# Expert stage of a 32-expert layer: the down bias is summed once from the gate table, turned h goes ahead of the turned rows, and the next expert's bias is added between them

## The reference

```python
gates = jax.nn.softmax(top_vals, axis=-1)            # 4 of 32 per token
gu = xb @ w_gu[e] + b_gu[e]                          # 1024 -> 2048
gate = jnp.minimum(gu[:, :D_FF], SWIGLU_LIMIT)
up = jnp.clip(gu[:, D_FF:], -SWIGLU_LIMIT, SWIGLU_LIMIT)
h = (up + 1.0) * (gate * jax.nn.sigmoid(SWIGLU_ALPHA * gate))
y_row = h @ w_down[e] + b_down[e]                    # 1024 -> 1024
y = segment_sum(y_row * gate_of_row, token)
x = layernorm(DEEPNORM_ALPHA * x + y, ln2_g, ln2_b)
```

## Time and profile before

| | us |
|---|---|
| median of 3 runs (lowest, highest) | 1252.86 (1252.75, 1255.14) |
| the profiled execution, its own time | 1254.36 |
| its span in the profile | 1252.6 |
| mean granted clock of TensorE | 0.985 |

### The profile page before, as it was taken

How to read it: one execution, slowest core, us unless ns; L and a number is a source line. 1 busy time by engine, 2 the same in 40 slices (tenths; PEclk the granted TensorE clock), 3 DMA queues, 4 the chain that set the end, 5 groups by cost and what they waited for, 6 DMA issues and landing times.

```text
span 1252.6 us, 14341 instructions
## 1 busy us (share of the span) xinstructions
PE 1192.6 (95%) x5761; PEld 564.6 (45%) x5761; DVE 521.7 (42%) x988; ACT 252.9 (20%) x392; POOL 13.4 (1%) x16
## 2 busy tenths in 40 slices
PE   9999999998999999999999998999999999999992
PEld 8989999563333333333333332333333333333330
DVE  5887788563223322223333222322332222333326
ACT  4645646111111111111111111111111111111101
POOL 1000000000000000000000000000000000000003
PEclk9999999999999999999999999999999999999986
DMA  9756645856999999999999999999999999999951
GB/s 246 233 185 208 195 134 152 322 204 269 384 422 421 421 420 421 421 420 421 422 421 421 421 420 422 421 421 421 421 420 422 422 420 421 421 421 421 421 226 42
DMA packets 120186, 443.73 MB, mean 354 GB/s; under 512 B 10824, under 2 KB 68312, under 8 KB 70974
## 3 DMA queue, kind: packets, MB, share of 16 engines
q1 hardware_dynamic: 120030, 442.69, 88.9%
q10 hardware_dynamic: 96, 0.22, 0.0%
HBM read 441.34 MB, written 1.53 MB: 354 GB/s over the span
## 4 chain that ended last, share of the span: by engine, by line
PE 79%; DVE 11%; ACT 7%; issue 3%; DMA 1%; DVEq 0%; POOL 0%; ACTq 0%; POOLq 0%
PE PS L758 36%; PE PS L790 18%; PE PS L699 7%; PE PS L614 5%; PE PS L632 2%; PE PS L707 2%; PE PS L714 2%; DVE w_lo L827 2%; PE PS L752 2%; DVE tiles L865 2%; ACT mid L526 2%; ACT mid L530 2%; ACT mid L548 1%; PE PS L785 1%; DVE tiles L929 1%
## 5 line engine op out<-in xcount | busy, mean ns | idle before, releaser
L758 PE MATMUL PS<-ring,mid 128*64 128x512 f32 x2048 | 447.6, 595 | 0.0
L758 PEld LDWEIGHTS PS<-ring,mid 128*64 128x64 f32 x2048 | 144.4, 137 | 286.9 <-issue 286.9
L790 PE MATMUL PS<-ring,mid 128*64 128x512 f32 x1024 | 230.6, 603 | 0.0
L1121 DVE TENSOR_SCALAR PS<-PS 128x512 f32<-128x512 f32 x32 | 22.4, 699 | 384.5 <-PE PS L758 384.5
L614 PE MATMUL PS<-x_hi,w_hi 128*128 128x320 f32 x448 | 141.7, 316 | 3.8 <-DVE w_lo L827 3.8
L1108 DVE TENSOR_TENSOR ys<-PS,ys 64x512 fp32r<-64x512 f32 x64 | 44.1, 689 | 235.3 <-ACT ys L551 234.9
L614 PE MATMUL PS<-x_hi,w_lo 128*128 128x320 f32 x448 | 139.1, 310 | 0.0
L614 PE MATMUL PS<-x_lo,w_hi 128*128 128x320 f32 x448 | 139.0, 310 | 0.0
L790 PEld LDWEIGHTS PS<-ring,mid 128*64 128x64 f32 x1024 | 71.6, 139 | 139.3 <-issue 139.3
L865 DVE SCALAR_TENSOR_TENSOR x_tok<-PS,gate,x_tok 128x1024 f32<-128x1024 f32 (+1 forms) x96 | 122.9, 1281 | 27.4 <-PE PS L721 24.3
L543 ACT ACTIVATE mid<-PS 128x512 f32<-128x512 f32 x32 | 19.1, 597 | 454.6 <-DVE PS L1121 454.6
(11 more groups left out here) (195 smaller groups left out, 700.1 us busy)
## 6 DMA issues: line engine op xcount, KB each, us to landing
ring<-in_w_gu SPq DMA_DIRECT2D x256, 1024.0 KB, 20.9
ring<-in_w_down SPq DMA_DIRECT2D x128, 1024.0 KB, 20.9
raw<-in_w_in SPq DMA_DIRECT2D x56, 512.0 KB, 5.2
ring<-in_w_out SPq DMA_DIRECT2D x4, 1024.0 KB, 6.1
x_tok<-in_x_prompt SPq DMA_DIRECT2D x1, 1024.0 KB, 6.9
out<-x SPq DMA_DIRECT2D x2, 512.0 KB, 2.6
bias_raw<-in_b_gu SPq DMA_DIRECT2D x4, 128.0 KB, 3.2
ln_g<-in_ln_g SPq DMA_DIRECT2D x1, 512.0 KB, 4.1
```

Source lines behind the costliest of these rows:

```text
L758: last = mm(PS[64 * a:64 * a + 64, b, :], xgT[:, u % 4, u // 4, :], w[:, o:o + HALF], start=False, stop=(u == KC - 1))
L790: last = mm(PS[64 * a:64 * a + 64, XB, :], hT[:, 2 * (u % 2) + j, u // 2, :], w[:, j * D + a * HALF:j * D + (a + 1) * HALF], start=False, ...
```

## The change

- The matmul of down bias in each expert goes (L785), and the down product starts its sum with its own first matmul. For it, `gate4` (four copies of the gate table) is written by VectorE before the routing's list of extra blocks is formed, turned by TensorE (three transposes) and split in a high part `gT_hi` (ScalarE) and a low part `gT_lo` (VectorE). In expert 0, where there is nothing to combine, `gated_bias` multiplies it with b_down, four matmuls for each of the three tiles, and `begin` on VectorE writes ALPHA times x1 plus that product into `y_acc`.
- `turn_h` comes ahead of `turn_x`. `turn_x` now waits for ScalarE's copy of turned h, which goes to `th` itself.
- `add_bias` for the next expert stands between the two turns and not at the head of the expert, except for experts 0, 14 and 16 (`ALONE`).
- `keep_busy` before and after the first `turn_x` goes; the wait for posT moves into expert 0, behind its gate/up product; the register loads of TensorE, ScalarE and VectorE move behind expert 13.
- VectorE does three adds in every expert, expert 0 among them, so the counts of `c_done` and `c_taken` move by three.

```diff
             def one_expert(i, it):
 
                 s, n = i % 2, UNITS * i
+
+                def sum_up(t):
+
+                    if i == 0:
+                        gated_bias(t, CB[t])
+                    else:
+                        combine(t, 1 - s, CB[t])
+
                 pe.wait_ge(xgT_ok, 2 * it + rows_in(i))
-                sel = esel4[:, s].rearrange("p a r -> p (a r)")
-                for b in range(2):
-                    mm(PS[:, b, :], sel, bias4[:, b, :], start=True, stop=False)
+                if i in ALONE:
+                    add_bias(s)
...
-                if i > 0:
-                    if i > 1:
-                        pe.wait_ge(c_taken, 6 * it + 3 * (i - 1))
+                if i == 0:
+                    pe.wait_ge(gT_ok, 2)
+                else:
+                    pe.wait_ge(c_taken, 6 * it + 3 * i)
                     pe.wait_ge(ohT_ok, 2 * it + i)
-                    combine(2, 1 - s, CB[2])
+                sum_up(2)
                 pe.wait_ge(ohT_ok, 2 * it + (i + 1))
-                if i + 1 < NE:
-                    pe.wait_ge(xg_ok, 2 * it + (rows_in(i) + 1))
-                    turn_x(xg_sb, tx_done)
-                if i > 0:
-                    combine(1, 1 - s, CB[1])
-                if i + 1 < NE:
-                    pe.wait_ge(xgT_ok, 2 * it + (rows_in(i) + 1))
                 pe.wait_ge(h_ok, 2 * it + (i + 1))
                 turn_h(th, ht_done)
-                if i > 0:
-                    pe.wait_ge(c_taken, 6 * it + (3 * (i - 1) + 1))
-                    combine(0, 1 - s, CB[0])
+                sum_up(1)
+                if i + 1 < NE:
+                    if i + 1 not in ALONE:
+                        add_bias(1 - s)
+                    pe.wait_ge(xg_ok, 2 * it + (rows_in(i) + 1))
+                    pe.wait_ge(hT_ok, 2 * it + (i + 1))
+                    turn_x(xg_sb, tx_done)
+                pe.wait_ge(c_taken, 6 * it + (3 * i + 1))
+                sum_up(0)
                 pe.wait_ge(hT_ok, 2 * it + (i + 1))
-                mm(PS[:, XB, :], sel, bias4[:, 2, :], start=True, stop=False)
```

and the new product:

```diff
+            def gated_bias(t, bank):
+
+                t0, n = TILES[t]
+                for a in range(2):
+                    rows = slice(64 * a, 64 * a + 64)
+                    mm(PS[0:n, bank + a, :], gT_hi[rows, t0:t0 + n], bias4[rows, 2, :], start=True, stop=False)
+                    last = mm(PS[0:n, bank + a, :], gT_lo[rows, t0:t0 + n], bias4[rows, 2, :], start=False, stop=True)
+                last.then_inc(c_done, 1)
```

More of the change, by code:

```diff
@@ L27 @@
 LOOP = 14
+ALONE = (0, LOOP, LOOP + 2)
 AHEAD = 3
@@ L196, in hybrid_layer @@
         xg_sb, xgT_f = (mid[:, i * HALF:(i + 1) * HALF] for i in range(2))
-        th = mid[:, 4 * HALF:5 * HALF]
         ys = place("ys", [P, 2, HALF], MID + 8 * HALF, F32R)
@@ L203, in y_rows @@
             return ys[first:first + ROWS, a, :]
-        hT_f = xg_sb
+        th = mid[:, 4 * HALF:5 * HALF]
+        hT_f = th
+        gT_hi = place("gT_hi", [P, T], MID + 8 * HALF, F32R)
+        gT_lo = place("gT_lo", [P, T], MID + 8 * HALF + 4 * T, F32R)
+        gate4 = mid[:, 4 * HALF - 3 * P:4 * HALF].rearrange("p (t h e) -> p t h e", t=3, h=4)
         xgT = xgT_f.rearrange("p (j a r) -> p j a r", j=4, a=2)
@@ L255, in hybrid_layer @@
         pos_ok, pos_turned, posT_ok = sem("pos_ok"), sem("pos_turned"), sem("posT_ok")
+        g4_ok, gate_turned, gT_ok = sem("g4_ok"), sem("gate_turned"), sem("gT_ok")
         tab_ok, tab_done, items_ok = sem("tab_ok"), sem("tab_done"), sem("items_ok")
@@ L535, in _ @@
             act.activation(posT4[:, :], PS[:, 6, 0:T], ACT.Copy).then_inc(posT_ok, 1)
-            act.wait_ge(items_ok, 1)
-            n_loop = act.value_load(pairs[0:1, 0:1], min_val=1, max_val=1 + MAX_EXTRA // 2)
-            n_more = act.value_load(pairs[0:1, 1:2], min_val=0, max_val=MAX_EXTRA // 2)
+            act.wait_ge(gate_turned, 1)
+            act.activation(gT_hi[:, :], PS[:, 7, 0:T], ACT.Copy).then_inc(gT_ok, 1)
             def one_expert(i, it):
@@ L545, in one_expert @@
                     take_xg(2 * it + (rows_in(i) + 1))
-                    take_xgT(2 * it + (rows_in(i) + 1))
                 act.wait_ge(ht_done, 2 * it + (i + 1))
                 act.activation(hT_f, PS[:, TB, :], ACT.Copy, scale=0.5).then_inc(hT_ok, 1)
+                if i + 1 < NE:
+                    take_xgT(2 * it + (rows_in(i) + 1))
                 act.wait_ge(used, 2 * UNITS * it + UNITS * (i + 1))
@@ L554, in _ @@
                 one_expert(i, 0)
+            act.wait_ge(items_ok, 1)
+            n_loop = act.value_load(pairs[0:1, 0:1], min_val=1, max_val=1 + MAX_EXTRA // 2)
+            n_more = act.value_load(pairs[0:1, 1:2], min_val=0, max_val=MAX_EXTRA // 2)
             with act.Fori(0, n_loop) as it:
@@ L725, in _ @@
             gather(1)
+            pe.wait_ge(g4_ok, 1)
+            for t, (t0, n) in enumerate(TILES):
+                last = pe.transpose(PS[:, 7, t0:t0 + n], gate4[0:n, t], ident[0:n, 0:n])
+            last.then_inc(gate_turned, 1)
             pe.wait_ge(tab_ok, 1)
@@ L731, in _ @@
             last.then_inc(tab_done, 1)
-            keep_busy(2, 1)
             pe.wait_ge(xg_ok, 1)
             turn_x(xg_sb, tx_done)
-            keep_busy(2, 1)
             pe.wait_ge(pos_ok, 1)
@@ L744, in unit, with chosen, add_bias @@
                 return ring[:, n % SLOTS, :]
+            def chosen(par):
+                return esel4[:, par].rearrange("p a r -> p (a r)")
+            def add_bias(par):
+                for b in range(2):
+                    mm(PS[:, b, :], chosen(par), bias4[:, b, :], start=True, stop=False)
+            def gated_bias(t, bank):
[5 more added lines that the diff above has]
+                last.then_inc(c_done, 1)
             def one_expert(i, it):
                 s, n = i % 2, UNITS * i
+                def sum_up(t):
[3 more added lines that the diff above has]
+                        combine(t, 1 - s, CB[t])
                 pe.wait_ge(xgT_ok, 2 * it + rows_in(i))
-                sel = esel4[:, s].rearrange("p a r -> p (a r)")
-                for b in range(2):
-                    mm(PS[:, b, :], sel, bias4[:, b, :], start=True, stop=False)
+                if i in ALONE:
+                    add_bias(s)
                 for u in range(KC):
@@ L760, in one_expert @@
                     last.then_inc(used, 1)
-                mm(PS[:, TB, 0:T], sel, posT4[:, :], start=True, stop=True).then_inc(spread_done, 1)
+                if i == 0:
+                    pe.wait_ge(posT_ok, 1)
+                mm(PS[:, TB, 0:T], chosen(s), posT4[:, :], start=True, stop=True).then_inc(spread_done, 1)
                 if i > 0:
@@ L791, in one_expert @@
                                       w[:, j * D + a * HALF:j * D + (a + 1) * HALF],
-                                      start=False, stop=(u == 3 and j == 1))
+                                      start=(u == 0 and j == 0), stop=(u == 3 and j == 1))
                     last.then_inc(used, 1)
+            for i in range(LOOP):
+                one_expert(i, 0)
             pe.wait_ge(items_ok, 1)
@@ L797, in _ @@
             n_more = pe.value_load(pairs[0:1, 1:2], min_val=0, max_val=MAX_EXTRA // 2)
-            pe.wait_ge(posT_ok, 1)
-            for i in range(LOOP):
-                one_expert(i, 0)
             with pe.Fori(0, n_loop) as it:
@@ L811, in _ @@
             pe.wait_ge(ylo_ok, 2 * n_more + NE)
-            pe.wait_ge(c_taken, 6 * n_more + 3 * (NE - 1))
+            pe.wait_ge(c_taken, 6 * n_more + 3 * NE)
             for t, b in LAST_SUMS:
@@ L1059, in _ @@
             last.then_inc(pos_ok, 1)
+            dve.tensor_copy(gate4, gate[:, :, :].unsqueeze(2).to_broadcast([P, 3, 4, NE])).then_inc(g4_ok, 1)
             link(dve.tensor_scalar(ext, cnt, float(ROWS), None, ALU.is_gt))
@@ L1096, in part, with begin @@
                 return dve.value_load(items[0:1, 1, ds(i, 1)], min_val=0, max_val=NB)
[L1098 to L1102, removed]
+            def begin(t, count, bank):
+                n = TILES[t][1]
+                dve.wait_ge(c_done, count)
+                return stt(halves(y_acc[0:n, t, :]), halves(x1[0:n, t, :]), ALPHA, PS[0:n, bank:bank + 2, :],
+                           ALU.mult, ALU.add)
             def low_part(count):
@@ L1114, in one_expert @@
                 s = i % 2
-                if i > 0 and i != LOOP + 2:
+                if i == 0:
+                    dve.wait_ge(gT_ok, 1)
+                    dve.tensor_tensor(gT_lo[:, :], PS[:, 7, 0:T], gT_hi[:, :].bitcast(F32), ALU.subtract)\
+                       .then_inc(gT_ok, 1)
+                elif i != LOOP + 2:
                     low_part(2 * it + i)
@@ L1127, in one_expert @@
                 stt(th, up, 1.0, th, ALU.add, ALU.mult).then_inc(h_ok, 1)
-                if i > 0:
-                    for q, t in enumerate((2, 1, 0)):
-                        add(t, before, 6 * it + (3 * (i - 1) + q + 1), CB[t]).then_inc(c_taken, 1)
```

(13 more changed lines are left out.)

## The result

The changed kernel takes 1241.78 us in the median of four runs (1238.89 to 1242.78), the kernel before 1252.80 (1252.06 to 1255.14): 0.9905 of it by all its executions, interval 0.9883 to 0.9927. That is 11.0 us less by the medians and 11.9 by the ratio, where 17.4 were forecast. The median lies 0.3 us above the upper end of the forecast's range, 1241.5; 0.9905 of the 1252.86 that the forecast stood on is 1241.0, just inside it, and the interval runs from 1238.2 to 1243.7, across that end. The two profiled executions differ by more than the medians do: 1254.36 and 1241.01 us, spans 1252.6 and 1239.2, so 13.4 us.

A forecast was written before the change was run, and what follows sets the result against it. TensorE and the weight transfers both run at full load, TensorE living on a shrinking lead. Terms -14.4 - 0.8 - 1.6 - 0.6 = -17.4 us, from 1252.86 to 1235.5 us; range 1232.5 to 1241.5.

The forecast's parts named there:

- the lead, 14.4 us: At unit 379, last gate/up unit: TensorE's remaining lead over the weight transfers, read from bytes moved; pays out -14.4 us.
- the semaphore's release: At unit 379's landing: a small deduction that takes the lead from 14.6 to 14.4 us.
- The start, -0.8: Before the experts: the expert stage begins earlier despite gate4's extra copy; -0.8 us, bounds -1.3 and +0.5.
- The hole in expert 0, -1.6: Expert 0's transfer gap: gated_bias keeps TensorE busy, no clock fall, first down unit earlier; -1.6 us, bounds 0 and -2.7.
- The last expert, -0.6: Last expert, which has no gather: only the down bias matmul L785 goes; -0.6 us.
- The rule against it: Paced experts: by the Trainium skill's HAM oscillation rule, TensorE idling 0.78 us per gate unit would run them at a throttled clock.
- the second rival: Paced experts: the clock stays down, 52 us an expert; two whole experts give 1279 us; chance 3%.
- the first rival: After unit 379: its matmuls at half speed (+1.7) and all down matmuls at 1.2 GHz (+4.2), 1241.4 us; chance 12%.
- its signs: What would show it: last ring transfer near 1207.5, 421 GB/s, late experts 29.9 us, ring waits 30 to 45 us.

## Why the prediction was right and wrong

**Right: what bounds the kernel, and what stays of the gain.** That TensorE lives on a lead, that it would save 42 to 60 us and that only the lead would be paid out was the core of the forecast. TensorE's expert fell to 27.02 us (26.9 to 27.5 was said). Matmuls idle for the ring 30.7 us (30 to 45 was said), most late experts take 29.8 us (the transfers' 29.9 was said; two take 30.1 and 31.1), the rate stays 421, and with lighter transfers 46 us that were waits for weights come back as time saved. The lead is gone at expert 12, a little before the 14 to 20 that were said; the loop after expert 15, which the prediction left out, gives part of it back.

**Wrong in size: the lead, 14.4 us.** This is the step that failed. I took the landing of unit 379 from the bytes moved. What TensorE waits for is the last of its packets, on the slowest of the 16 DMA engines, and the mean of the engines is ahead of that one: in the kernel before the 16 landing marks of unit 379 come from 1190.8 to 1198.2, on average at 1195.0. A row of the kernel before that I didn't read had the answer: the times from issue to landing of the last two gate units, issued at 1168.2 and 1172.2.

```profile
DMA to landing us min/median/max: 26.0/26.7/27.5
```

The 27.5 belongs to the unit issued at 1168.2, the 26.0 to the last one. So unit 379 landed at 1198.2, and the lead was 1208.9 - 1198.2 = 10.7 us. Between the two executions unit 379's matmuls moved from 1208.9 to 1197.6, 11.2 us: the lead of 10.7 and 0.6 by which its landing came earlier (1197.6). The prediction's term is 3.7 us too large, and that is most of the 4.0 us that the forecast has too much on the spans (17.4 against 13.4). The 0.2 us it took off for the semaphore's release are 0.04 in the chain above (landed at 1197.59, used at 1197.63).

**The start, -0.8: not seen.** Its own piece is right in kind. From the product of the list of blocks to the first bias matmul 1.59 us pass (287.01 to 288.60), where 2.79 did:

```profile
286.44 0.57 PE PS L736 x3
287.01 0.23 PE PS L741 x4
...
287.95 0.60 ACT mid L535
...
288.60 0.73 PE PS L763 x2
```

But that product came 1.2 us later: 0.57 are the three new transposes, the rest lies before the change's first line. The prediction had the transposes on an idle TensorE; there is no such gap, since they follow the gather, which ends at 286.43, and the product follows them. Over the twelve profiled executions the first gate/up matmul comes anywhere between 287.8 and 294.8, and a run bound by the transfers carries each of these microseconds to its end. An effect of 0.8 can't be told in that; in the two executions that are compared here both begin the gate/up product at 289.3.

**The hole in expert 0, -1.6: -1.4 there, -0.6 at the end.** The stretches of the earlier trace rows, after:

```profile
305.00:310.00 5.00, 5.00 (x28) 2.48 (x26) 3.87 (x5) 1.62 (x3) 0.00 (x0) 1.00 1.01 426
310.00:315.00 5.00, 5.00 (x26) 1.73 (x26) 1.22 (x1) 0.17 (x1) 0.00 (x0) 1.00 0.95 364
315.00:320.00 5.00, 5.00 (x26) 1.63 (x24) 2.07 (x6) 1.18 (x2) 0.00 (x0) 1.00 1.00 341
```

TensorE is busy in the first, the clock doesn't fall in the second, and the loss is (57 + 80) x 5 = 0.69 MB or 1.6 us where it was 2.7. Unit 32 lands at 329.4, where it landed at 330.7: 1.4 us earlier. By unit 379 only 0.6 of that is left (1197.6 against 1198.2); where the rest went the traces don't say. All nine executions with gated_bias in expert 0 keep the clock there, and the three without it lose it.

**The last expert, -0.6: -0.5**, from unit 379's first matmul to the first down matmul. Not in the sum: the down stage 1.1 us shorter, since the clock fell for 3.4 us there and not for 6.8, and the tail 0.5 shorter, which I can't place. The first is luck: with three units in flight the kernel before had 3.4 us of fall there too. The sum as measured, on the spans: -10.7 (lead) - 0.6 (transfers) - 0.5 - 1.1 - 0.5 = -13.4. The 2.4 us between that and the medians' 11.0 is the scatter of single runs: this profiled run before stood 1.6 over its median, that of after 0.8 under.

**The rule against it.** TensorE did idle about 0.5 us before each paced unit, and over 100 us of paced experts the page of stretches says:

```profile
1100.00:1200.00 100.00, 92.14 (x412) 30.78 (x410) 26.50 (x39) 10.71 (x18) 0.00 (x0) 1.00 1.01 421
```

The granted clock is 1.00, so the second rival did not come true. The Trainium skill's warning on HAM oscillation (TensorE: Matmul & The Clock Gate) is of tiles of matmuls that are shorter than the wait between them. The prediction held the matmuls (1.71 us) against the whole transfer (2.49 us) and not against the wait. The wait is 0.5 us and so shorter than the matmuls: the paced experts don't meet the page's condition, and no run here tests its rule. The clock does fall, from 736.6 to 746.9, at the loop after expert 15, where TensorE has idled for 2.9 us before it.

The range, by the medians, missed by 0.3 us. Its upper end, 1241.5, was the price of the first rival, the clock down at the end. That the measured 1241.8 comes so near it is luck: unit 379's matmuls ran at a granted clock of 1.00 (1.94 us with their modelled ends) and the down stage took 8.3 us, not 13.7. The lead, on which most of the sum stood, was given no bounds of its own. And the prediction put the last ring unit at 1205.3 in its sum and near 1207.5 among its signs; it landed at 1207.5, 0.6 us before it did in the kernel before (1208.1).

## What to carry to other kernels

Where two resources both run at full load, find which one is living on a stock (a ring that began full) and how much is left at its last use: that is all that work taken off the faster one can bring. Measure that stock by issue and landing of the very transfer that is waited for, not by bytes moved, which run ahead of it (by 3.6 to 4.3 us here). Past that point spare time on the compute engine is free: here five extra matmuls an expert cost nothing, and ten cost 23 us.

## What the runs showed of the hardware

- The 16 parts of a transfer don't land together. With eleven units of 1 MB in flight unit 379 lands 4.3 us, 1.7 units, after the count of packets has reached it; with six 3.8 us, with three 1.6. Its landing marks spread over 8.5, 7.9 and 2.3 us. Holding the queue short takes the head start away and gains nothing. Whether one engine is always the slow one is not shown; the rows don't name the engines.
- Where `used` doesn't hold SP back, about eleven of these transfers are in flight (27.0 / 2.49): in the changed kernel, from 900 to 1000 issue to landing stays at 26 to 28 us, and an issue itself takes 2.07 us, where it takes 0.33 with six in flight.
- Idling of 0.5 us in every 2.5 leaves TensorE's granted clock at 1.00 (1100 to 1200). At the last down stage of the changed kernel, with a hole of 2.6 us before turned h, it fell to 1.2 GHz for 3.4 us in five of five executions; with 5, 10 or 12 filling matmuls in that expert it did not in three of three, nor in the one whose weights were never waited for.
